# The second expert table: 32 tiles loaded whole and multiplied by a weight matrix made on the chip, the other rows gathered, mostly behind the first table

## The reference

```
q = (h @ w_q) in 8 heads of two halves;  s1 = q1 . keys1,  s2 = q2 . keys2      # 128 keys each
v1, i1 = top_k(s1, 16);  v2, i2 = top_k(s2, 16)
best, pos = top_k(v1 + v2 over the 16 x 16 pairs, 16);  expert = (i1 * 128 + i2)[pos]
gates = softmax(best)
act = gelu(sum over d of u_tab[expert] * h)          # for each token, head and k
y[token] = sum over heads and k of gates * act * v_tab[expert]
out = rmsnorm(x + g2 * y)
```

## Time and profile before

| | |
|---|---|
| median of three executions | 1830.77 us |
| profiled execution, its span | 1830.54 us, 1827.9 us |
| bytes moved, mean rate | 716.51 MB, 392 GB/s |
| software queue (GpSimd's DMAs) | 604.02 MB |
| DVE busy | 1124.9 us (62%) |
| PE busy | 920.5 us (50%) |
| GpSimd busy | 745.0 us (41%) |
| ACT busy | 415.9 us (23%) |

### The profile page before, as it was taken

One profiled execution on the slowest core, in us unless ns is written; L12 is line 12 of the kernel. 1 busy time (PEld: TensorE's weight loads), 2 busy tenths in 40 slices (PEclk: granted clock), 3 DMA queues, 4 the chain that ended last, 5 costly groups with the idle time before them and its releaser, 6 DMA issues.

```text
span 1827.9 us, 14235 instructions
## 1 busy us (share of the span) xinstructions
PE 920.5 (50%) x4882; PEld 554.6 (30%) x4882; DVE 1124.9 (62%) x1555; ACT 415.9 (23%) x1215; POOL 745.0 (41%) x625
## 2 busy tenths in 40 slices
PE   2979999899898632232232222232422332332324
PEld 2649986888787500000000000000100000000001
DVE  5858886888789755545555555538455555554431
ACT  3004343853302411112111111112211202020110
POOL 0001111000064755545546555438645455555531
PEclk9989999999999866666665666666666566676667
DMA  9999998669699999999999999999999999999996
GB/s 338 386 389 405 397 353 319 254 229 366 259 402 414 421 421 422 421 421 422 422 421 422 422 421 421 422 406 393 423 421 423 421 422 422 422 421 422 422 395 276
DMA packets 138249, 716.51 MB, mean 392 GB/s; under 512 B 11159, under 2 KB 15437, under 8 KB 63693
## 3 DMA queue, kind: packets, MB, share of 16 engines
q0 software_dynamic: 82976, 604.02, 80.1%
q1 hardware_dynamic: 55212, 111.77, 16.6%
HBM read 713.65 MB, written 2.10 MB: 392 GB/s over the span
## 4 chain that ended last, share of the span: by engine, by line
DMA 39%; PE 30%; POOL 15%; issue 7%; DVE 6%; ACT 3%; SPq 1%; DVEq 0%; POOLq 0%; ACTq 0%
DMA v_rows<-in_peer_v,expert_rows 29%; PE ps L1032 9%; POOL u_rows L670 8%; POOL v_rows L670 7%; PE ps L934 5%; PE ps L999 4%; PE ps L777 4%; DVE first_acc L461 3%; DMA u_rows<-in_peer_u,expert 3%; DMA ring<-in_w_peer_q 2%; PE ps L771 2%; DMA ada_first<-in_w_ada 2%; DMA u_rows<-in_peer_v,expert_rows 1%; PE ps L432 1%; PE ps L311 1%
## 5 line engine op out<-in xcount | busy, mean ns | idle before, releaser
L1784 DVE SCALAR_TENSOR_TENSOR u_rows<-u_rows,h 128x2048 f32<-128x2048 f32 x256 | 587.1, 2293 | 516.4 <-DMA u_rows<-in_peer_u,expert 513.7
L1032 PE MATMUL ps<-v_rows,diag 128*32 128x512 f32 x1984 | 357.0, 885 | 819.7 <-DMA v_rows<-in_peer_v,expert_rows 655.4
L670 POOL DMA_INDIRECT v_rows<-in_peer_v,expert_rows x248 | 328.9, 1326 | 452.3 <-PE ps L1032 393.6
L670 POOL DMA_INDIRECT u_rows<-in_peer_u,expert x256 | 369.2, 1442 | 144.3 <-issue 74.5
L1032 PEld LDWEIGHTS ps<-v_rows,diag 128*32 128x32 f32 x1984 | 85.4, 155 | 1089.7 <-issue 971.7
L286 POOL DMA_DIRECT2D ada_late<-in_w_ada x61 | 32.3, 530 | 307.2 <-DVE ada_acc L300 264.2
L300 DVE SCALAR_TENSOR_TENSOR ada_acc<-ada_late,cact,ada_acc 128x2048 f32<-128x2048 f32 x57 | 133.9, 2349 | 18.2 <-DMA ada_late<-in_w_ada 17.1
L1329 ACT COPY weight_rows<-hidden 32x4 f32<-32x4 f32 x256 | 50.2, 196 | 363.0 <-DVE hidden L1792 360.2
L1312 ACT ACTIVATE hidden<-hidden 128x16 f32<-128x16 f32 x16 | 3.5, 216 | 533.0 <-DVE u_rows L1784 533.0
L999 PE MATMUL ps<-h2T,ring 128*128 128x256 f32 x512 | 117.8, 391 | 6.5 <-DMA ring<-in_w_peer_q 6.5
L999 PEld LDWEIGHTS ps<-h2T,ring 128*128 128x128 f32 x512 | 99.8, 197 | 20.6 <-DMA ring<-in_w_peer_q 6.9
(11 more groups left out here) (274 smaller groups left out, 1342.4 us busy)
## 6 DMA issues: line engine op xcount, KB each, us to landing
ada_late<-in_w_ada POOLq DMA_DIRECT2D x61, 1024.0 KB, 7.9
ada_first<-in_w_ada SPq DMA_DIRECT2D x64, 512.0 KB, 11.6
ring<-in_w_in SPq DMA_DIRECT2D x10, 2048.0 KB, 23.8
ring<-in_w_o SPq DMA_DIRECT2D x8, 2048.0 KB, 16.7
ring<-in_w_peer_q SPq DMA_DIRECT2D x8, 2048.0 KB, 16.5
opened<-in_w_in SPq DMA_DIRECT2D x8, 1024.0 KB, 12.8
u_rows<-in_peer_u,expert POOLq DMA_INDIRECT x256, 20.2
v_rows<-in_peer_v,expert_rows POOLq DMA_INDIRECT x248, 19.7
```

Source lines behind the costliest of these rows:

```text
L670: nc.gpsimd.indirect_dma_start(buf[:, :], None, table, bass.IndirectOffsetOnAxis(ap=places, axis=0)).then_inc(done, 16)
L1032: ins = nc.tensor.matmul(ps[rows, k, :], diag[(QUADS * g + c) % len(diag)][:, :], bufs[c][:, 512 * k:512 * k + 512], start=first, stop=last)
L1784: nc.vector.scalar_tensor_tensor(out=buf[:, :], in0=buf[:, :], scalar=1.0, in1=h2[:, q // H, :], op0=ALU.mult, op1=ALU.mult, accum_out=hid ...
```

## The change

In the second table the last 32 of 128 tiles (i1 of 96 and up) are no longer gathered. They are loaded whole, 32 loads of 1 MiB from SP, and multiplied by a dense weight matrix `dense_weight[t]` (128 rows of the tile x 128 tokens for each of the 32 tiles) for each half t of the tokens. All other picks are gathered as before, by the same 256 indirect DMAs with a bound: a row whose index lies above the bound is not fetched. Its weight in the diagonals is set to zero (`kept`), so what the buffer holds there does not count.

The dense weights are made on the chip. `slots_to_partitions` transposes i1, i2 and the weights so that a token's 128 picks lie on the partitions. For eight tokens at a time (`one_hot`, 16 batches for each half) DVE compares i2 with 0 to 127 and i1 with 96 to 127, and multiplies the second by the weight in two parts that together carry it to full precision. PE multiplies the two one-hot matrices, two matmuls of 32 columns for each token (`scattered`), and ACT copies the result out transposed.

The order of the expert stage is another. The u gathers come first, one a slot, with a v gather after every fifth from slot 30 on, so that 44 v gathers (11 groups) lie among them; the one-hot batches of half 0 stand at slots 134 to 194, one in four slots. All other v gathers follow the last u gather. After the last dot PE makes half 1's dense weights, with eight row groups between, then the rows of the final gain and of g2, then 32 dense tiles with 41 row groups between them, and last four row groups. The two halves now have four PSUM banks each, and both are finished at the end, half 0 beside the last row groups. There are six u buffers (seven before), three sets of four v buffers (two before; the third takes over u buffers when the dots are done) and three dense buffers.

```diff
+HALF_SLOTS = SLOTS // TT
+HALF_GROUPS = HALF_SLOTS // QUADS
+ALL_GROUPS = SLOTS // QUADS
+DENSE = 32
+SPARSE = NK - DENSE
+BATCH = 8
+BATCHES = P // BATCH
...
+    u_rows = [at(f"u_rows{b}", o, [P, D]) for b, o in enumerate(
+        (A + 64 * KB, A + 72 * KB, A + 80 * KB, B + 16 * KB, B + 24 * KB, A + 88 * KB))]
+    v_rows = [[at(f"v_rows{b}_{c}", o, [P, D]) for c, o in enumerate(places)] for b, places in enumerate((
+        [A + 8 * c * KB for c in range(4)], [A + (32 + 8 * c) * KB for c in range(4)],
+        (A + 80 * KB, A + 88 * KB, B + 16 * KB, B + 24 * KB)))]
+    dense_rows = [at(f"dense_rows{b}", o, [P, D]) for b, o in enumerate((A + 64 * KB, A + 72 * KB, C + 16 * KB))]
+    dense_weight = [at(f"dense_weight{t}", o, [P, DENSE, P]) for t, o in enumerate((A + 112 * KB, B))]
...
+    EARLY_GROUPS = 11
+    FIRST_V, V_STEP = 30, 5
+    BUILD_GROUPS = 8
+    LAST_GROUPS = 4
+
+    def group_key(g):
+        return FIRST_V + 2 + QUADS * V_STEP * (g + 1)
+
+    def batch_key(b):
+        return HALF_SLOTS + 6 + 4 * b
+
+    def row_set(g):
+
+        if g < EARLY_GROUPS:
+            return g % 2, g // 2
+        early = [len(range(i, EARLY_GROUPS, 2)) for i in range(2)] + [0]
+        k = g - EARLY_GROUPS
+        b = (EARLY_GROUPS % 2, 1 - EARLY_GROUPS % 2, 2)[k % 3]
+        return b, early[b] + k // 3
 
...
+
+    def dense_groups(i):
+
+        n = ALL_GROUPS - EARLY_GROUPS - BUILD_GROUPS - LAST_GROUPS
+        lo = EARLY_GROUPS + BUILD_GROUPS
+        return range(lo + n * i // DENSE, lo + n * (i + 1) // DENSE)
 
...
                     load_half(sp, f"w_pq{n}", half, wpq_view, 512 * n)
+            for i in range(DENSE):
+                b, use = i % len(dense_rows), i // len(dense_rows)
+                if i == 0:
+                    sp.wait_ge(dots, SLOTS)
+                if i == 2:
+                    full(sp, f"dw1_{BATCHES - 1}")
+                if use:
+                    sp.wait_ge(dense_used, i - len(dense_rows) + 1)
+                lo = NK * (SPARSE + i)
+                sp.dma_start(dense_rows[b][:, :], peer_v[0][lo:lo + NK, :]).then_inc(dense_landed[b], 16)
...
+            last_sparse = pool.to_reg(NK * SPARSE - 1)
...
+                g, c = divmod(n, QUADS)
+                q, m = divmod(g, GROUPS)
+                b, use = row_set(g)
...
-                elif n < LAST and n >= len(v_rows) and c == 0:
-                    group_used(pool, n // QUADS - 2)
-                gather(expert_rows[:, q, m, c:c + 1], buf, landed, peer_v[0])
+                if n == 0:
+                    full(pool, "p7")
+                if c == 0 and b == 2 and use == 0:
+                    pool.wait_ge(dots, SLOTS)
+                if c == 0 and use:
+                    pool.wait_ge(v_used[b], use)
+                nc.gpsimd.indirect_dma_start(v_rows[b][c][:, :], None, peer_v[0], bass.IndirectOffsetOnAxis(
+                    ap=expert_rows[:, q, m, c:c + 1], axis=0), bounds_check=last_sparse, oob_is_err=False).then_inc(v_landed[b], 16)
 
             given = 0
-            for n in range(SLOTS + TOPK):
-                if n < SLOTS:
-                    gather_u(n)
-                while given < n + 1 - TOPK - max(0, min(14, 15 - n // TOPK)):
+            for n in range(SLOTS):
+                gather_u(n)
+                if given < QUADS * EARLY_GROUPS and n == FIRST_V + V_STEP * given:
                     gather_v(given)
                     given += 1
+            for n in range(QUADS * EARLY_GROUPS, SLOTS):
...
-
+            def row_group(g):
+
+                b, use = row_set(g)
+                first = g == 0
+                if first:
+                    for name in ("sc6", "sc7", "h2_7"):
+                        copied(pe, name)
+                    pe.wait_ge(ada_bias, 8)
+                pe.wait_ge(v_landed[b], 16 * QUADS * (use + 1))
+                pe.wait_ge(diagonal, QUADS * (g + 1))
+                t, last = g // HALF_GROUPS, g == ALL_GROUPS - 1
                 for k in range(4):
-                    if g == 0:
-                        copied(pe, f"g2b{k}")
-                    if g == HALF_GROUPS:
...
                     for c in range(QUADS):
                         rows = slice(QUAD * c, QUAD * c + QUAD)
-                        ins = nc.tensor.matmul(ps[rows, k, :], diag[(QUADS * g + c) % len(diag)][:, :],
-                                               bufs[c][:, 512 * k:512 * k + 512], start=first, stop=last)
+                        ins = nc.tensor.matmul(ps[rows, 4 - 4 * t + k, :], diag[(QUADS * g + c) % len(diag)][:, :],
+                                               v_rows[b][c][:, 512 * k:512 * k + 512], start=first, stop=last, skip_group_check=True)
                     if last and k < 3:
                         ins.then_inc(summed, 1)
-                mark_used(ins, g)
...
+            def scattered(t, b):
+                bank = take(pe, f"dw{t}_{b}")
+                i = BATCHES * t + b
+                pe.wait_ge(one_hots, i + 1)
+                for k in range(BATCH):
+                    o = bank[:, DENSE * k:DENSE * k + DENSE]
+                    nc.tensor.matmul(o, low_hot[i % 2][:, k, :], high_hot[0][i % 2][:, k, :], start=True, stop=False)
+                    ins = nc.tensor.matmul(o, low_hot[i % 2][:, k, :], high_hot[1][i % 2][:, k, :], start=False, stop=True)
+                fill(ins, f"dw{t}_{b}")
...
+            def dense(i):
+                b, use = i % len(dense_rows), i // len(dense_rows)
+                if i == 0:
+                    for g in range(4):
+                        copied(pe, f"g2b{g}")
+                pe.wait_ge(dense_landed[b], 16 * (use + 1))
+                for t in range(TT):
+                    for k in range(4):
+                        ins = nc.tensor.matmul(ps[:, 4 - 4 * t + k, :], dense_weight[t][:, i, :], dense_rows[b][:, 512 * k:512 * k + 512],
+                                               start=i == 0 and t == 1, stop=i == DENSE - 1 and t == 0, skip_group_check=True)
+                        if i == DENSE - 1 and t == 0:
+                            ins.then_inc(summed, 1)
+                ins.then_inc(dense_used, 1)
+
+            early = 0
+            for n in range(SLOTS):
+                if n == HALF_SLOTS + 3:
+                    slots_to_partitions(0)
+                if n in (batch_key(b) + 2 for b in range(BATCHES)):
+                    scattered(0, (n - 2 - batch_key(0)) // 4)
+                if early < EARLY_GROUPS and n == group_key(early):
+                    row_group(early)
+                    early += 1
+            slots_to_partitions(1)
+            for b in range(BATCHES):
+                scattered(1, b)
+                if b % 2:
+                    row_group(EARLY_GROUPS + b // 2)
+            spread_row("fg", vcB, 38)
+            spread_row("g2b", modc, G2)
+            for i in range(DENSE):
+                dense(i)
+                for g in dense_groups(i):
+                    row_group(g)
+            for g in range(ALL_GROUPS - LAST_GROUPS, ALL_GROUPS):
+                row_group(g)
 
...
+            def next_diagonals(g):
+                if g + GROUPS < ALL_GROUPS:
+                    group_used(act, g)
+                    diagonals_of(g + GROUPS)
...
+                d = hidden[:, q, :]
+                step(nc.vector.scalar_tensor_tensor(out=d, in0=d, scalar=gate_sum[:, q:q + 1], in1=gate[:, q % 4, :],
+                                                    op0=ALU.mult, op1=ALU.mult))
+                if q >= 2:
+                    dve.wait_ge(weights_spread, q - 1)
+                nc.vector.scalar_tensor_tensor(out=kept[:, q % 2, :], in0=halves[:, q // H, 0, q % H, :], scalar=float(SPARSE), in1=d,
...
+            def one_hot(t, b):
+
+                i, tokens = BATCHES * t + b, slice(BATCH * b, BATCH * b + BATCH)
+                if i >= 2:
+                    full(dve, f"dw{(i - 2) // BATCHES}_{(i - 2) % BATCHES}")
+                column = lambda a, n: a[:, tokens].unsqueeze(2).broadcast_to([P, BATCH, n])
+                row = lambda a, n: a.unsqueeze(1).broadcast_to([P, BATCH, n])
+                high, low = high_hot[0][i % 2], high_hot[1][i % 2]
+                step(nc.vector.tensor_tensor(low[:, :, :], row(iota128[:, SPARSE:NK], DENSE), column(slot_rows[:, 0, :], DENSE), ALU.is_equal))
+                nc.vector.tensor_tensor(low_hot[i % 2][:, :, :], row(iota128[:, :], NK), column(slot_rows[:, 1, :], NK), ALU.is_equal)
+                step(nc.vector.tensor_tensor(high[:, :, :], low[:, :, :].bitcast(F32), column(weight_high[:, :].bitcast(F32), DENSE), ALU.mult))
+                nc.vector.tensor_tensor(low[:, :, :], low[:, :, :].bitcast(F32), column(weight_low[:, :], DENSE),
+                                        ALU.mult).then_inc(one_hots, 1)
 
...
+                if n == HALF_SLOTS + 5:
+                    weight_parts(0)
+                if n in (batch_key(b) for b in range(BATCHES)):
+                    one_hot(0, (n - batch_key(0)) // 4)
 
...
```

(11 more changed lines are left out.)

264 lines of the change are left out of this document (122 added, 142 removed).

## The result

The changed kernel takes **1835.74 us** in the median (1827.59 to 1842.64, 20 runs), the kernel before on the same chips 1828.72 (1824.72 to 1833.84): ratio 1.0037, interval 1.0025 to 1.0049. It is slower by 0.4%, a small loss, but the whole interval lies above 1. Forecast were 1830 and no change. So stages are compared by their lengths.

A forecast was written before the change was run, and what follows sets the result against it. DMA bytes bound the expert stage before the change. Last dot 1325, plus build 4.5 + 61 + 7 + 13 to 1410, loop 403 to 1813, 4 + 9.9 to 1827, 2.6 around it: 1830 us, no change; range 1780 to 1900.

The forecast's parts named there:

- Skipped rows free: Second table's gathers: a skipped row costs no transfer, so a v gather takes 1.85 us, 473 us for 637.
- DVE's sum 778.6 plus 34: First stage: DVE's own work of 778.6 us from 512.6, plus 34 of smaller costs; last dot ends at 1325.
- blocked gathers: First stage: DVE waits on late u rows for 18 v gathers that find GpSimd blocked, 17 us, bounds 0 and 77.
- small terms: First stage: last 32 slots short of DMA +10, six u buffers for seven +2, uneven landings +5 us.
- Rival A: Faster: gathers slip in free among the dots and DMA never stands in the second stage; 1780 us, chance 0.17.
- B's 77: Slower rival: blocked gathers cost the dots 77 us instead of 17; 1890 us, chance 0.18.
- Build 85: Between last dot and dense loop: 4.5 gelu to transposes, 61 half 1's weights and row groups, 7 cold start, 13 final rows.
- 403 us, so DMA is last, PE 92% busy: Dense loop: DMA needs 382 us of bytes, +9 and +12, together 403; PE's 372 us is earlier.
- the pause: Dense loop: transfers lose 9 us until the first freed set is issued again.
- Unevenness: Dense loop: rows skipped unevenly over the DMA engines add 12 us, range 0 to 30.
- rival D: Slower: PE falls to 1.2 GHz in the dense loop, +341 us; 2171 us, chance 0.04.
- Tail: After the last group's first product: 4 us in the forecast's sum, then 9.9 to the end, unchanged.

The follow-up runs named there:

- m1_skip_price: A kernel of gathers alone, 12 buffers, 60 gathers a phase, with growing shares of rows skipped: a skipped row costs 0.01 us of one engine, a fetched one 0.31.
- e4_few_early: Changed kernel with 3 instead of 11 row groups gathered behind the first table (32 v gathers moved to the later stage): 1875.3 us.
- e1_half_dense: Changed kernel with half of the dense products of 30 of the 32 dense tiles left out, loads and gathers kept: 1824.5 us in one run.
- e5_even_skips: Changed kernel with the second table's row numbers from a made table, so every fourth partition skips in each gather: 1824.1 us.
- e6_even_half: Changed kernel with e5_even_skips and e1_half_dense together: evenly spread skips and halved dense products: 1817.6 us.
- v9: Changed kernel with 16 dense tiles instead of 32, a fourth set of four v rows and one dense buffer instead of three: 1834.0 us.
- v10: v9 with 16 early row groups instead of 11 (one v gather every 3 dots) and one last group instead of four: 1813.7 us.
- e2_no_bound: Changed kernel with the bound put at the end of the table, so every row of a v gather is fetched: 1944.5 us in one run.

## Why the prediction was wrong, step by step

**Skipped rows free: right.** 0.01 us for 0.31 (m1_skip_price). The gathered bytes fell by 69 MB, as the forecast's 164 us (637 - 473) have it, and the 36 MB "in all" come out at 35.3 (716.51 to 681.18).

**Dots, DVE's sum 778.6 plus 34: right in its mechanism, 10 us too long.** Measured 802.2, with 786.9 at 3 early groups. DVE was busy 744.87 us of 802.3, 93%. The blocked gathers (17, bounds 0 and 77; the forecast's own 18 x 0.9 gives 16) are 15.3 for 32 of the 44. What was too much stands in the small terms (the last 32 slots 10, buffers 2, unevenness 5): all of them, with the other 12 gathers, are 8.3 in e4_few_early. Rival A's free gathers and B's 77 are both excluded by that run. One sign misled: the share of the DMA engines was forecast at 0.9 and is 0.98, which looks like a bound by transfers. But they moved 385 GB/s, 91% of 422, at that share. Read the GB/s, not the share.

**Build 85: right in sum, by luck in its pieces.** 86.2. The forecast took the high clock "as PE has no gap here". These windows of the build say otherwise (columns as in the earlier trace rows):

```profile
1325.20:1340.00 14.80, 14.80 (x78) 9.70 (x78) 6.99 (x12) 1.70 (x6) 6.00 (x5) 0.57 1.02 417
1340.00:1360.00 20.00, 20.00 (x121) 10.62 (x120) 9.65 (x16) 2.70 (x10) 8.34 (x7) 0.66 0.97 382
1360.00:1380.00 20.00, 20.00 (x182) 13.16 (x186) 13.36 (x22) 4.86 (x18) 13.17 (x12) 1.00 0.90 337
```

PE is busy without a gap from 1325.2 on, and the granted clock is 0.57, then 0.66, and 1.00 only from 1360. The first three row groups took 6.5, 6.2 and 5.9 us instead of 3.4, and the first two batches 0.21 us a load. Later batches took 0.11 a load, 1.8 each where 2.1 was forecast, and with the 7 us for the cold start the sum came out. The transfers did not stand for 20 us: they ran at 381 GB/s over the build, 8 us below full.

**Dense loop "403 us, so DMA is last, PE 92% busy": this step failed.** It is 420.8, 18 more. The transfers were last, as forecast, but two terms of the sum were mis-sized. The forecast added 382 us of bytes, 9 for the pause until the first freed set is issued again and 12 for skipped rows that fall unevenly on the engines, and put the meeting of PE and transfers at nothing.

- Bytes: 391 instead of 382. These two lines of the changed kernel are the whole loop and its first 25 us:

```profile
1405.00:1827.00 422.00, 391.91 (x1924) 138.21 (x1928) 8.48 (x15) 47.21 (x191) 167.01 (x168) 0.97 0.98 391
1405.00:1430.00 25.00, 24.18 (x103) 9.25 (x104) 0.00 (x0) 5.51 (x25) 5.93 (x6) 1.00 0.82 305
```

  391 GB/s over 422 us are 165.0 MB. The forecast counted 161: it had all three sets and the dense buffers filled when the loop begins, while gathers issued up to 1401.78 still landed in it, and 1 MB of the result is stored in it.
- PE: 7 instead of 0 (e1_half_dense has 22 us above its bytes instead of 29). PE had 376 us of work in 391, 96% and not 92, as a dense tile took 7.1 us and a group 3.6, not 6.85 and 3.41. The rule that failed is that of the later of two rates: what is earlier on average was priced at nothing.
- Unevenness: 11 for the 12 taken (e5_even_skips has 18 us above its bytes instead of 29). This term was right.
- What neither takes away: 12 (e6_even_half), of which 5 stand at the start, where the changed kernel has 7: GpSimd's gathers stop for 14.02 us until PE frees a set. That is the pause, for which 9 were taken. 3 stand at the end and 3 between. The skipped rows' own cost is about 3.5 (167 gathers, some 5,500 skipped rows, 0.01 us, over 16 engines).

So the 18 are 9 of bytes, 7 of PE, and 2 in the rest. Why PE's work costs 7 us while it is the earlier side is argued, not shown: row groups become ready unevenly, and with three sets each side in turn waits for the other, as the rows around 1533 show once. That a longer queue would take it away was not tested with 32 tiles. Each of these figures rests on one profile.

By the Trainium skill, DMA: Bandwidth & Descriptors, section The descriptor swizzle, the forecast's estimate for unevenness was 8 us against the 12 taken. e5_even_skips shows 11 above the bytes of the loop and 11.6 in the time, nearer the 12; the profile doesn't list the load of each engine, so the map itself is not shown.

**Clock: right in the loop.** 0.98, so rival D falls. Its argument, that a PE which is busy throughout goes with the high clock, doesn't hold as it stands, as the windows of the build show. **Tail: right**, 14.2 us from the last group's start against 13.9.

That the forecast came near was in part luck: 10 too much for the dots stood against 18 too little for the loop, with 1 for the build and 5 for a first dot that was late in the profiled run. Against the median, 1835.7, the forecast of 1830 was 5.7 us low, and it said "no change" where the kernel lost 0.4%.

## What to carry to other kernels

When bytes are taken out of a stage bound by transfers, price the stage by what comes next (here DVE in the dots, PE in the loop). Where PE has nearly as much work as the transfers take (here 376 us in 391) and the queue between them is short, don't price the earlier one at nothing: here it cost 7 us in 400, and rows that fall unevenly on the engines another 11. Count as bytes of a stage also what was issued before it and lands in it. And transfers belong in the stage that has room for them: five more row groups gathered behind the dots, with one last group for four, gained 20 us (v9 to v10), where going from 16 to 32 tiles loaded whole gained nothing.

## What the hardware showed beyond that

- A gather whose row numbers exceed the bound still makes one packet for each skipped row, at 0.01 us of an engine (m1_skip_price), and GpSimd's part gets no shorter: 0.99 us with a bound, whether it skips or not, 0.94 without. With the 0.30 between two, a gather that fetches half of its rows or fewer is bound by GpSimd at 1.29 us.
- Which partitions skip matters: at nearly the same number of skipped rows (8,192 and 8,453), an even pattern moved 416 GB/s, the routing's 402.
- The profile's "HBM read" is not what was fetched. It counts skipped rows in full: 747.20 MB both for the changed kernel and for e2_no_bound, although the queues moved 681.18 and 750.39 MB, and 377.49 MB (360 gathers of 1.0486) for m1_skip_price, which moved 222.42. Whether the chip reads a skipped row and drops it, these runs don't tell; a whole 1.0486 MB every 1.29 us would be 813 GB/s, nearly twice the 423 seen.
